# The first norm token tile by token tile inside the first projection, and the S5 poles at its twelfth output

## The reference, cut to what matters

```
xn   = x * rsqrt(mean(x*x, axis=-1) + 1e-6) * norm_mix_pre     # 512 x 1024
proj = xn @ w_in                                               # 1024 x (2304 + 800 + 2048)
...
# second block, S5 mixer, per (group, state): the poles
lr = minimum(lam_re, -1e-4); dt = exp(log_dt)
mag = exp(lr*dt); ab_re = mag*cos(li*dt); ab_im = mag*sin(li*dt)
cf_re, cf_im = ((ab - 1) / (lr + i*li))
```

## Time and profile before

| | |
|---|---|
| median of three executions | 1818.64 us (1817.35 to 1818.89) |
| the profiled execution | 1817.56 us, its span 1815.8 us |
| PE busy | 1625.5 us, 90% of the span |
| PE weight loads | 1304.4 us, 72% |
| DVE, ACT, POOL busy | 824.4, 554.6 and 258.8 us |
| mean granted TensorE clock | 0.91 of full |

### The profile page before, as it was taken

One profiled execution on the slowest core, in us unless ns is written; L12 is line 12 of the kernel. 1 busy time (PEld: TensorE's weight loads), 2 busy tenths in 40 slices (PEclk: granted clock), 3 DMA queues, 4 the chain that ended last, 5 costly groups with the idle time before them and its releaser, 6 DMA issues. The chain is left out here.

```text
span 1815.8 us, 18388 instructions
## 1 busy us (share of the span) xinstructions
PE 1625.5 (90%) x7364; PEld 1304.4 (72%) x7364; DVE 824.4 (45%) x1214; ACT 554.6 (31%) x837; POOL 258.8 (14%) x272
## 2 busy tenths in 40 slices
PE   3998899668979899999998999389977899999997
PEld 3886677566767788888876667355776688888886
DVE  4222333346654544333454762464674534323334
ACT  4221233424443422222334211334122423212222
POOL 0000000000021696000011763000220200000000
PEclk9999999888999999999998999655567899999999
DMA  3222011220022222232222221100001222322222
GB/s 134 93 93 96 32 62 48 81 70 1 1 70 82 93 93 93 96 108 98 93 93 79 70 70 60 41 23 1 1 1 47 70 93 99 110 93 93 93 81 93
DMA packets 34634, 129.23 MB, mean 71 GB/s; under 512 B 4549, under 2 KB 18781, under 8 KB 22133
## 3 DMA queue, kind: packets, MB, share of 16 engines
q1 hardware_dynamic: 32964, 127.24, 20.3%
q10 hardware_dynamic: 1584, 0.81, 0.2%
HBM read 124.82 MB, written 3.17 MB: 70 GB/s over the span
## 5 line engine op out<-in xcount | busy, mean ns | idle before, releaser
L223 DVE TENSOR_TENSOR ring_lo<-ring_raw,ring_hi 128x2048 fp32r<-128x2048 f32 (+5 forms) x115 | 265.5, 2313 | 254.9 <-ACT ring_hi L213 254.7
L242 PE MATMUL bank<-xT_hi,ring_hi 128*128 128x512 f32 (+1 forms) x864 | 343.6, 398 | 5.0 <-PEq L1126 3.3
L242 PE MATMUL bank<-xT_hi,ring_lo 128*128 128x512 f32 (+1 forms) x864 | 340.2, 394 | 0.0
L242 PE MATMUL bank<-xT_lo,ring_hi 128*128 128x512 f32 (+1 forms) x864 | 340.1, 394 | 0.0
L213 ACT CAST ring_hi<-ring_raw 128x2048 fp32r<-128x2048 f32 (+5 forms) x115 | 212.6, 1852 | 277.7 <-DMA ring_raw<-in_w_ff 131.1
L242 PEld LDWEIGHTS bank<-xT_hi,ring_hi 128*128 128x128 f32 (+1 forms) x864 | 164.2, 190 | 45.1 <-issue 9.9
L242 PEld LDWEIGHTS bank<-xT_hi,ring_lo 128*128 128x128 f32 (+1 forms) x864 | 163.5, 189 | 35.8
L242 PEld LDWEIGHTS bank<-xT_lo,ring_hi 128*128 128x128 f32 (+1 forms) x864 | 163.7, 189 | 34.3
L242 PE MATMUL bank<-ring_hi,hid_hi 128*128 128x512 f32 x432 | 169.9, 393 | 4.1 <-DVE ring_lo L223 4.1
L242 PE MATMUL bank<-ring_lo,hid_hi 128*128 128x512 f32 x432 | 169.4, 392 | 0.0
L242 PE MATMUL bank<-ring_hi,hid_lo 128*128 128x512 f32 x432 | 169.2, 392 | 0.0
(11 more groups left out here) (434 smaller groups left out, 2303.8 us busy)
## 6 DMA issues: line engine op xcount, KB each, us to landing
ring_raw<-in_w_ff SPq DMA_DIRECT2D x32, 1024.0 KB, 4.8
ring_raw<-in_w_up SPq DMA_DIRECT2D x22, 1024.0 KB, 4.9
ring_raw<-in_w_proj SPq DMA_DIRECT2D x8, 1024.0 KB, 5.1
ring_raw<-in_w_gates SPq DMA_DIRECT2D x8, 1024.0 KB, 4.9
ring_raw<-in_w_out SPq DMA_DIRECT2D x8, 1024.0 KB, 4.8
ring_raw<-in_w_fm SPq DMA_DIRECT2D x12, 512.0 KB, 4.8
ring_raw<-in_w_dn_a SPq DMA_DIRECT2D x6, 1024.0 KB, 4.9
ring_raw<-in_w_proj SPq DMA_DIRECT2D x8, 512.0 KB, 5.0
```

Source lines behind the costliest of these rows:

```text
L223: k.nc.vector.tensor_tensor(k.ring.lo[:, g % SLOTS, 0:n], k.raw[:, g % SLOTS, 0:n], plain(k.ring.hi[:, g % SLOTS, 0:n]), ALU.subtract).the ...
L242: mm = k.nc.tensor.matmul(out, x, y, start=first and n == 0, stop=last and n == 3 * len(pairs) - 1)
```

## The change

A class `Opening` takes the place of the first two blocks, and its work is done inside the block of the first projection.

- SP issues x, chunks 0 to 2, then the nine other constants; ACT issues only `cols` and `ident`.
- The gain is spread to a row on all partitions: PE turns eight columns of `cols`, each broadcast to 128 x 128, into banks 0 and 1, and ACT copies them to `op_gain`.
- The norm goes token tile by token tile: ACT squares, DVE adds eps, POOL takes the power, DVE scales the tile and multiplies with the gain row in one operation, PE turns it in two half banks, ACT writes the high part, DVE the low part. PE turns tiles 0 and 1 ahead of step 0, tile 2 ahead of step 1 and tile 3 ahead of step 2.
- Chunks 0 and 1 are split between these operations (`split_hi(k, act, 1)`, `split_hi(k, act, 2)` and their counterparts on DVE).
- The poles are done by `act_each` and `dve_each` at j = 12.

The diff, without its empty added lines:

```diff
--- before.py
+++ after.py
@@ -270,35 +270,156 @@
         self.eng.wait_ge(self.s.sem, self.s.base)
 
 
-def stage_load(k):
-    nc, d = k.nc, k.d
-    poles_act, poles_dve = s5_poles(k)
-    cols_in = k.sig("cols_in")
-    with nc.Block() as block:
-        @block.sync
-        def _(sp):
-            for t in range(T):
-                sp.dma_start(k.h[:, t, :], d["x"][t * P:(t + 1) * P, :]).then_inc(k.x_in[t].sem, 16)
-            issue_chunks(k, sp, SLOTS)
-        @block.scalar
-        def _(act):
-            act.dma_start(k.cols[:, :], d["cols"]).then_inc(cols_in.sem, 16)
-            for dst, name in ((k.ident[:, :], "ident"),
-                              (k.identb[:, :], "identb"), (k.mask_band[:, :], "mask_band"),
-                              (k.mask_d4[:, :], "mask_d4"), (k.mask_d16[:, :], "mask_d16"),
-                              (k.mask_row[:, :], "mask_row"), (k.mask_col[:, :], "mask_col"),
-                              (k.mask_lev[:, :, :], "mask_lev"), (k.ropeA[:, :, :, :], "ropeA"),
-                              (k.ropeB[:, :, :], "ropeB")):
-                act.dma_start(dst, d[name]).then_inc(k.c_in.sem, 16)
-            act.wait_ge(cols_in.sem, 16)
-            poles_act(act)
-        @block.vector
-        def _(dve):
-            dve.wait_ge(cols_in.sem, 16)
-            poles_dve(dve)
+class Opening:
+    def __init__(self, k, at):
+        self.k = k
+        self.gain = k.sb("op_gain", at[0], [P, D])
+        self.xn = k.sb("op_xn", at[1], [P, 2, D])
+        self.junk = k.sb("op_junk", at[2], [P, D])
+        self.poles_act, self.poles_dve = s5_poles(k)
+        self.ms, self.rs, self.half = k.stat[:, 0:2 * T], k.stat[:, 2 * T:3 * T], k.stat[:, 3 * T:3 * T + 1]
+        (self.cols_in, self.ident_in, self.spread, self.gained, self.sumsq, self.mean, self.root, self.scaled, self.turned,
+         self.high, self.low) = (k.sig("op_" + n) for n in (
+             "cols", "ident", "spread", "gained", "sumsq", "mean", "root", "scaled", "turned", "high", "low"))
+    def banks(self, t):
+        return [self.k.pb[4 + t % 2 * 2 + c] for c in range(2)]
+    def sync(self, sp):
+        k, d = self.k, self.k.d
+        for t in range(T):
+            sp.dma_start(k.h[:, t, :], d["x"][t * P:(t + 1) * P, :]).then_inc(k.x_in[t].sem, 16)
+        issue_chunks(k, sp, SLOTS)
+        consts = ((k.identb[:, :], "identb"), (k.mask_band[:, :], "mask_band"),
+                  (k.mask_d4[:, :], "mask_d4"), (k.mask_d16[:, :], "mask_d16"),
+                  (k.mask_row[:, :], "mask_row"), (k.mask_col[:, :], "mask_col"),
+                  (k.mask_lev[:, :, :], "mask_lev"), (k.ropeA[:, :, :, :], "ropeA"),
+                  (k.ropeB[:, :, :], "ropeB"))
+        for dst, name in consts:
+            sp.dma_start(dst, d[name]).then_inc(k.c_in.sem, 16)
+        sp.wait_ge(k.c_in.sem, 16 * len(consts))
+    def turn(self, pe, t):
+        k = self.k
+        if t >= 2:
+            pe.wait_ge(self.low.sem, self.low.base + 2 * (t - 2) + 2)
+        pe.wait_ge(self.scaled.sem, self.scaled.base + t + 1)
+        for f in range(KD):
+            mm = k.nc.tensor.transpose(self.banks(t)[f // 4][:, f % 4 * P:f % 4 * P + P],
+                                       self.xn[:, t % 2, f * P:(f + 1) * P], k.ident[:, :])
+            if f % 4 == 3:
+                mm.then_inc(self.turned.sem, 1)
+    def pe(self, pe, t):
+        k = self.k
+        if t == 0:
+            pe.wait_ge(self.cols_in.sem, 16)
+            pe.wait_ge(self.ident_in.sem, 16)
+            for f in range(KD):
+                mm = k.nc.tensor.transpose(k.pb[f // 4][:, f % 4 * P:f % 4 * P + P],
+                                           col(k, "mix_pre", f).to_broadcast([P, P]), k.ident[:, :])
+                if f % 4 == 3:
+                    mm.then_inc(self.spread.sem, 1)
+            self.turn(pe, 0)
+        if t + 1 < T:
+            self.turn(pe, t + 1)
+        if t == 0:
+            pe.wait_ge(self.gained.sem, 2)
+        pe.wait_ge(self.low.sem, self.low.base + 2 * t + 2)
+    def act(self, act):
+        k, nc = self.k, self.k.nc
+        act.dma_start(k.cols[:, :], k.d["cols"]).then_inc(self.cols_in.sem, 16)
+        act.dma_start(k.ident[:, :], k.d["ident"]).then_inc(self.ident_in.sem, 16)
+        def square(t):
+            act.wait_ge(k.x_in[t].sem, 16)
+            if t:
+                act.wait_ge(self.sumsq.sem, self.sumsq.base + t)
+            nc.scalar.activation(self.junk[:, :], k.h[:, t, :], ACT.Square, scale=1.0 / 32,
+                                 accum_out=self.ms[:, t:t + 1]).then_inc(self.sumsq.sem, 1)
+        def high_part(t):
+            for c in range(2):
+                act.wait_ge(self.turned.sem, self.turned.base + 2 * t + c + 1)
+                nc.scalar.copy(k.xT.hi[:, 4 * c:4 * c + 4, t * P:(t + 1) * P],
+                               self.banks(t)[c][:, :].rearrange("p (f e) -> p f e", f=4)).then_inc(self.high.sem, 1)
+        square(0)
+        for c in range(2):
+            act.wait_ge(self.spread.sem, c + 1)
+            nc.scalar.copy(self.gain[:, 512 * c:512 * c + 512], k.pb[c][:, :]).then_inc(self.gained.sem, 1)
+        square(1)
+        square(2)
+        high_part(0)
+        split_hi(k, act, 1)
+        high_part(1)
+        square(3)
+        split_hi(k, act, 2)
+        high_part(2)
+        high_part(3)
+    def pool(self, pool):
+        for t in range(T):
+            pool.wait_ge(self.mean.sem, self.mean.base + t + 1)
+            self.k.nc.gpsimd.tensor_tensor(self.rs[:, t:t + 1], self.ms[:, T + t:T + t + 1], self.half,
+                                           ALU.pow).then_inc(self.root.sem, 1)
+    def dve(self, dve):
+        k, v = self.k, self.k.nc.vector
+        def mean(t):
+            dve.wait_ge(self.sumsq.sem, self.sumsq.base + t + 1)
+            v.tensor_scalar(self.ms[:, T + t:T + t + 1], self.ms[:, t:t + 1], EPS, None, ALU.add).then_inc(self.mean.sem, 1)
+        def scale(t):
+            dve.wait_ge(self.root.sem, self.root.base + t + 1)
+            if t >= 2:
+                dve.wait_ge(self.turned.sem, self.turned.base + 2 * (t - 1))
+            v.scalar_tensor_tensor(out=self.xn[:, t % 2, :], in0=k.h[:, t, :], scalar=self.rs[:, t:t + 1],
+                                   in1=self.gain[:, :], op0=ALU.mult, op1=ALU.mult).then_inc(self.scaled.sem, 1)
+        def low_part(t):
+            for c in range(2):
+                dve.wait_ge(self.high.sem, self.high.base + 2 * t + c + 1)
+                v.tensor_tensor(k.xT.lo[:, 4 * c:4 * c + 4, t * P:(t + 1) * P],
+                                self.banks(t)[c][:, :].rearrange("p (f e) -> p f e", f=4),
+                                plain(k.xT.hi[:, 4 * c:4 * c + 4, t * P:(t + 1) * P]),
+                                ALU.subtract).then_inc(self.low.sem, 1)
+        Chain(dve, k.sig("dve_chain"))(v.memset(self.half, -0.5))
+        mean(0)
+        dve.wait_ge(self.gained.sem, 2)
+        scale(0)
+        mean(1)
+        scale(1)
+        mean(2)
+        low_part(0)
+        scale(2)
+        split_lo(k, dve, 1)
+        low_part(1)
+        mean(3)
+        scale(3)
+        split_lo(k, dve, 2)
+        low_part(2)
+        low_part(3)
+    def poles(self, who):
+        def each(eng, j):
+            if j == 12:
+                (self.poles_act if who == "act" else self.poles_dve)(eng)
+        return each
 
 
 def stage_norm_T(k, tag, src, width, gain, dst, xn_kb, arrive=None, sync=None):
@@ -388,7 +509,7 @@
 
 
 def stage_gemm(k, steps, evac, owner=None, act_each=None, dve_each=None, dve_tail=None, pool=None,
-               needs=(), closing=None):
+               needs=(), closing=None, opening=None):
 
 
 
@@ -416,6 +537,8 @@
     with nc.Block() as block:
         @block.sync
         def _(sp):
+            if opening is not None:
+                opening.sync(sp)
             if closing is not None:
                 closing.sync(sp, release[n - 1])
             else:
@@ -425,6 +548,8 @@
         def _(pe):
             seen = set()
             for i, (g, j, out, pairs, first, last) in enumerate(steps):
+                if opening is not None and i < T:
+                    opening.pe(pe, i)
                 if g not in seen:
                     seen.add(g)
                     wait_chunk(k, pe, g)
@@ -446,6 +571,8 @@
 
         @block.scalar
         def _(act):
+            if opening is not None:
+                opening.act(act)
             split_hi(k, act, chunks[0] + LEAD)
             for j in range(n):
                 split_hi(k, act, fin[j] + LEAD)
@@ -462,6 +589,8 @@
 
         @block.vector
         def _(dve):
+            if opening is not None:
+                opening.dve(dve)
             split_lo(k, dve, chunks[0] + LEAD)
             for j in range(n):
                 if dve_each is not None:
@@ -484,6 +613,8 @@
 
         @block.gpsimd
         def _(eng):
+            if opening is not None:
+                opening.pool(eng)
             if pool is not None:
```

(5 more changed lines are left out.)

## The result

The changed kernel took 1804.24 us (median of four executions, 1803.04 to 1806.47) against 1818.07 for the kernel before: a ratio of 0.9928, with a 95% interval of 0.9915 to 0.9940. Timed once more with five executions (run `again`) it came to 0.9939 (0.9926 to 0.9951). So the change gains 11 to 14 us. I had forecast 5.5 and a range down to 9.1. The direction was right and the size wrong by a factor of two or more.

The account below looks back on a forecast made before the run. PE, 90% busy, bounds the kernel, except at the start, where it waits for the norm's chain. -14.1 + 8.6 = -5.5 us takes 1817.56 to 1812.1; the median's 1.1 more gives 1813.1, range 1809.5 to 1816.8.

Parts of the forecast that it names:

- What bounds the start, and that PE bounds the rest of the projection: Before the first weight product DVE's own list bounds; from there PE does, at 10.89 us a chunk.
- the signs: Trace marks to look for: first weight product at 17 to 19 us, step 4 at 33 to 35, about 7 us without PE.
- Gain 14.1 us: Start of the projection: 17.5 us from an earlier first product, less 3.4 for two turns between steps.
- the turn of tile 2 (8 x 0.207, 1.7 with its gap): Opening, between steps 0 and 1: PE turns tile 2 in 1.7 us.
- its twin: Opening, between steps 1 and 2: PE turns tile 3, also in 1.7 us.
- Slower: the clock stays low in the opening: Rival: low clock for nearly everything before step 4, products 7.2 us and turns 3.3 dearer, 1823.6 us; chance 0.06.
- Loss 8.6 us: Poles at j = 12: PE waits 6.9 us for chunk 7's low part, then 1.67 more at low clock.
- the rival with hidden poles: Poles at j = 12 cost nothing, as DVE and ACT idle 5 to 7 us at a time; 1804.5 us, chance 0.05.
- The clock: Low at PE's first product and again after the stall at the poles, 1.67 us each.
- The table load more: Rival: one more ACT table load before the first Exp at j = 12; loss 9.9 us, time 1814.4, chance 0.15.
- The early split of chunk 1 and the move of the constants, at nothing: Opening: chunk 1 split by 23.7 us without delay; nine constants on SP behind chunk 2, costing nothing.
- After the projection everything is as it was, moved: All code behind the projection keeps its length and only shifts in time; no gain or loss there.

Follow-up runs that it names:

- lo_first: The changed kernel, with DVE splitting chunks 7 and 8 before it begins the poles at j = 12; 1798.07 us, ratio 0.9900.
- split_late: `lo_first` without the two lines that split chunk 1 inside the opening, so it is split behind it; 1796.73 us, ratio 0.9891.
- consts_act: `lo_first` with the nine other constants issued by ACT behind `ident`, as before the change; 1799.39 us, ratio 0.9897.
- the nudges: `lo_first` with a DVE memset of 8 or 256 columns, for which PE waits, ahead of the last turning; 1799.95 and 1799.41 us.
- poles_alone: The kernel before, with only its poles moved from the first block to j = 12 of the projection; 1816.94 us, ratio 1.0002.

## Why the prediction was wrong

By its own steps:

- **What bounds the start, and that PE bounds the rest of the projection:** right. PE runs without gaps from 17.22 to 97, and the first product came at 17.22, as the signs had it (17 to 19). Step 4, at 31.6, came earlier than the 33 to 35 given there.
- **The opening, "Gain 14.1 us":** right in mechanism, too small by 2.2 (by 1.6 and 1.4 in `again` and `lo_first`). The first product came at 17.22, not 17.9 (the power took 0.54 where I had 0.65, `ident` landed 0.2 earlier; the scale was 1.28 where I had 1.29). The larger part is the term "the turn of tile 2 (8 x 0.207, 1.7 with its gap)" and its twin: they measured 0.8 us each, 1.8 us less together. 0.207 was the pitch of turns at the low clock. I had taken it for the full clock because the profile gave 1.00 there. The rival "Slower: the clock stays low in the opening" doubles the same 0.207 and is too dear by that.
- **The poles, "Loss 8.6 us":** right in place, order and kind, 7.6 measured. The idle time was 5.97 rather than 6.9, since the cast of chunk 8 began 6.1 us after chunk 5's end (the copy of output 11 starts at 86.22) and not 6.7; the slow clock behind it cost 1.6, where I had 1.67. The chain from Exp to the last DVE operation was 6.68, against 6.69. `lo_first` shows the cause. That the measured 1804.24 is the number of the rival with hidden poles (1804.5) is chance: they were not hidden.
- **The clock:** low at both starts, as forecast. PE had stood 2.99 us before 17.22 and 5.97 before 103.03; step 0 took 4.42 us, where I had 4.39.
- **The table load more (the first rival):** none came; the Exp at 94.09 follows the cast at once. The Trainium skill's rule (ScalarE activation tables: per-element evaluation and per-set limits, Table sets in the compiler and the runtime) agrees with this: the load at 1.66 served the squares, the copies and this Exp. The load inside the chain cost 1.30 from its start to the next activation (96.73 to 98.03), as in the earlier trace rows, and not the 2.66 of the Trainium skill's page ScalarE: Activation LUTs, What ACT_TABLE_LOAD costs, which no run here shows.
- **The early split of chunk 1 and the move of the constants, at nothing:** right within what the times can tell (`split_late`, `consts_act`).
- **"After the projection everything is as it was, moved":** this step failed. 3.3 us were gained there, in five stretches, because DVE's instruction list had become three instructions longer. `pad3` gains the same with three idle memsets alone, and the traces of the nudges have the largest part of it turned back. Up to the end of the projection the first trace was 8.7 ahead, still inside the range that I had given (9.1); this step carried the time out of it.

The sum of what was measured: -16.3 + 7.6 - 3.3 = -12.0, against -11 to -14 in the two timings and -11.2 and -13.3 in the two traces. The two mis-sized terms make 3.2 us of the difference to my 5.5, the failed step 3.3. What stays open: why DVE loses 0.35 us at that place of its list (no run here tells it), what made `consts_act` take the long form, and how much of the stretch at 295 to 335, which took 40.0 us in the kernel before, `pad3` and the changed kernel's first trace, and 36.9 to 40.0 elsewhere, is luck and how much follows from the shift; it may explain why `poles_alone` came out even rather than 0.9 slower. The best versions are `lo_first` and `split_late`, 6 to 9 us below the two timings of the changed kernel.

## What to carry to other kernels

When work is hung into a loop on two engines that hand to each other, look at what each has queued in front of it and behind it: here ACT's share came behind a cast that waits for a transfer, and DVE's ahead of the split that TensorE needed, and splitting ahead of the poles instead of behind them was worth 8 us. Take the price of a TensorE operation only from a stretch whose clock is recorded at both ends, or check it against the known spacing. And before a difference of 0.2% is put down to an edit, run the old kernel with a few idle instructions added: the end of the program moved by as much here, with nothing changed that matters.

## What was not expected of the hardware

- Three idle 128x1 memsets on DVE at the start made the kernel 3.2 us faster (ratio 0.9982). The DVE operation behind a wait at number 1087 of the engine's full recorded list is 0.35 us late, in all eleven traces in which a wait stands there. ACT has such a place at number 1087 of its own list (0.28 us, twelve traces), and DVE one more at 447 (0.38 us, the two traces with a wait there).
- With TensorE's restart 0.3 us later relative to the clock's last fall (45.35 against 45.05) the clock stayed at 0.50 for 5.9 us and not 2.7, and fell once more in the next products: 2.3 us for 0.3. The distance alone doesn't foretell the form: 45.10 was short in one trace and 45.11 long in another.
- Turns of 128x128 float32 start 0.21 us apart at the low clock and 0.11 at the full one; the profile gives 1.00 for a stretch ahead of its first clock record, whatever the clock was.
